# Stick-breaking scores of both heads from array rows 0 to 63 and 64 to 127, by chunks, with a changed start and mLSTM order

## The reference, cut to what matters

```
# mLSTM, 4 heads: keys and queries of 128, values of 256 (chunkwise in the reference)
s = einsum('bhts,...', qb, kb) * d
num = s @ v ;  den = sum(s) ;  h = num / max(abs(den), exp(-m)) ;  then rms_norm over the head, a gate, @ w_out

# stick-breaking, 16 heads of 64
z = einsum('bhtd,bhsd->bhts', qb, kb) * scale
log_1m = where(strict, log_sigmoid(-z), 0)
suffix = cumsum(log_1m, axis=3, reverse=True) - log_1m
a = where(strict, exp(log_sigmoid(z) + suffix), 0) ;  o = a @ v ;  o @ w_out
```

## Time and profile before

| what | us |
|---|---|
| median of 3 runs (2336.14 to 2337.36) | 2336.24 |
| the profiled execution's own time | 2334.94 |
| its span in the trace | 2333.6 |
| PE busy in the span | 2297.6 (98%) |
| DVE, ACT, POOL busy | 1042.0, 891.3, 1104.6 |

### The profile page before, as it was taken

The page is one execution under the profiler, slowest core; times in us unless marked ns, Lnnn a source line. Parts: engine busy times, 40 slices in busy tenths (PEclk is TensorE's granted clock), DMA queues, the critical chain, the costliest instruction groups (busy, mean ns, idle before and its releaser), DMA issues.

```text
span 2333.6 us, 31191 instructions
## 1 busy us (share of the span) xinstructions
PE 2297.6 (98%) x12833; PEld 1968.5 (84%) x12833; DVE 1042.0 (45%) x1521; ACT 891.3 (38%) x1322; POOL 1104.6 (47%) x833
## 2 busy tenths in 40 slices
PE   8999999999999999999999999999999999999998
PEld 6776888888888987778888888889999999999887
DVE  3138745622210614766564222018676446755402
ACT  4335643522222424746434222225345234322321
POOL 5335844444445352058335444555445444544453
PEclk9999999999999999999999999999999999999999
DMA  4222412222233242324123322323112222222232
GB/s 166 86 68 73 162 64 82 91 91 99 91 104 103 91 140 84 82 91 163 55 73 108 98 92 99 100 91 118 64 46 68 87 94 88 91 93 98 93 107 73
DMA packets 69054, 219.68 MB, mean 94 GB/s; under 512 B 9840, under 2 KB 14064, under 8 KB 68912
## 3 DMA queue, kind: packets, MB, share of 16 engines
q1 hardware_dynamic: 64160, 214.26, 28.2%
q10 hardware_dynamic: 4752, 3.42, 0.5%
HBM read 207.29 MB, written 2.10 MB: 90 GB/s over the span
## 4 chain that ended last, share of the span: by engine, by line
PE 92%; DVE 5%; ACT 2%; issue 1%; DMA 0%; SPq 0%; DVEq 0%; ACTq 0%
PE ps L443 76%; PE ps L572 6%; PE ps L958 2%; PE ps L996 1%; PE ps L737 1%; PE ps L761 1%; DVE x L1701 1%; DVE sp_lo L2139 1%; DVE ps L1699 1%; PE ps L467 1%; DVE u_lo L1680 1%; DMA w_land<-in_units 0%; DVE sp_hi L2137 0%; PE ps L658 0%; DVE arena L2135 0%
## 5 line engine op out<-in xcount | busy, mean ns | idle before, releaser
L2407 POOL TENSOR_TENSOR w_lo<-w_land,w_hi 128x512 fp32r<-128x512 f32 x768 | 1045.2, 1388 | 1106.3 <-ACT w_hi L1093 1105.5
L443 PE MATMUL ps<-u_hi,w_hi 128*128 128x512 f32 (+3 forms) x2360 | 755.0, 346 | 13.2 <-DVE u_lo L1680 12.8
L443 PE MATMUL ps<-u_lo,w_hi 128*128 128x512 f32 (+3 forms) x2360 | 750.9, 344 | 0.0
L443 PE MATMUL ps<-u_hi,w_lo 128*128 128x512 f32 (+3 forms) x2360 | 748.3, 343 | 0.0
L1093 ACT ACTIVATE w_hi<-w_land 128x1024 fp32r<-128x1024 f32 x384 | 401.1, 1051 | 249.6 <-DMA w_land<-in_units 247.0
L443 PEld LDWEIGHTS ps<-u_hi,w_hi 128*128 128x128 f32 x2360 | 420.2, 188 | 76.9 <-DVE u_lo L1680 15.3
L443 PEld LDWEIGHTS ps<-u_lo,w_hi 128*128 128x128 f32 x2360 | 417.8, 188 | 56.3 <-issue 1.4
L443 PEld LDWEIGHTS ps<-u_hi,w_lo 128*128 128x128 f32 x2360 | 418.5, 188 | 55.2
L443 PE MATMUL ps<-hid_hi,w_hi 128*128 128x512 f32 (+1 forms) x594 | 220.2, 371 | 0.0
L443 PE MATMUL ps<-hid_lo,w_hi 128*128 128x512 f32 (+1 forms) x594 | 219.7, 370 | 0.0
L443 PE MATMUL ps<-hid_hi,w_lo 128*128 128x512 f32 (+1 forms) x594 | 219.4, 369 | 0.0
(11 more groups left out here) (376 smaller groups left out, 3140.3 us busy)
## 6 DMA issues: line engine op xcount, KB each, us to landing
w_land<-in_units SPq DMA_DIRECT2D x384, 512.0 KB, 3.3
x<-in_xT SPq DMA_DIRECT2D x4, 528.0 KB, 7.1
arena<-in_memT ACTq DMA_DIRECT2D x2, 1024.0 KB, 5.3
outT<-x SPq DMA_DIRECT2D x16, 128.0 KB, 1.7
sb_split<-sb_split SPq DMA_DIRECT2D x14, 128.0 KB, 2.7
sb_q_lo<-sb_q_lo SPq DMA_DIRECT2D x13, 128.0 KB, 2.3
sb_split<-sb_q_lo SPq DMA_DIRECT2D x8, 128.0 KB, 2.4
sb_k_lo<-sb_split SPq DMA_DIRECT2D x6, 128.0 KB, 3.3
```

The costliest lines, as they stand in the source:

```text
L443: ins = pe.matmul(ps[:, bank, at:at + c1 - c0], w, rhs(k, c0, c1)[which], start=first and h == 0, stop=last and h == 2)
L2407: pool.tensor_tensor(w_lo[:, u % LAND, half], w_land[:, u % LAND, half], w_hi[:, u % RING, half].bitcast(F32), ALU.subtract).then_inc(*uni ...
```

## The change

**Start.** The first two units and x are loaded in smaller pieces, in the order in which they are needed: a half of unit 0, a tile of x, a half of unit 1, and so on; ACT's own queue loads the vectors. ACT rounds the halves between tiles of x, POOL subtracts them by halves, and PE's `first_head` takes unit 1 two tiles behind unit 0. Ahead of it PE multiplies zeros six times.

**mLSTM.** The three additions of `weights_sum` go from POOL to DVE; PE does the next head's scores and the sum of squares of the head before between the two halves of a numerator; the decays' arguments of heads 2 and 3 are made earlier, into a buffer of their own; DVE's and ACT's steps of the norm change places around this.

**Stick-breaking.** Nothing is stacked any more: the 63 copies by SP and their waits go, and `z` forms three products for every pair, of rows 0 to 63 for head 0 and 64 to 127 for head 1, alternating from one matmul to the next. For pairs 1 to 7 the work goes by chunks of both heads: PE does chunk 0 of both, then chunk 1 of both; ACT's exponentials go in that order; `z` waits for the exponentials of a chunk of both heads. POOL takes the two additions of head 1 and the rounding copies of chunk 1 of both heads.

```diff
+CHAIN = ((slice(SB_AT[2] + P, SB_AT[2] + 2 * P), slice(SB_AT[3], SB_AT[3] + P)),
+         (slice(SB_AT[1] + P, SB_AT[1] + 3 * P), slice(SB_AT[2], SB_AT[2] + 2 * P)))
...
+WARM = 6
+X_LOADS = ((0,), (1,), (2,), (3,), (4,), (5,), (6, 7))
+X_LOAD = (0, 1, 2, 3, 4, 5, 6, 6)
...
-        STACKED = {0: split_hi[0:4], 1: split_hi[4:8], 3: u_tiles(6) + u_tiles(7), 4: split_hi[0:4], 5: split_hi[4:8],
...
+        NATURAL = [split_hi[2 * i:2 * i + 2] for i in range(4)] + [u_tiles(i) for i in range(4, SB_H // 2)]
...
+            def first_head(name):
+                u0, u1 = UNIT[name], UNIT[name] + 1
+                begun[0] = 3
+                for k in range(UT):
+                    if k >= 2:
+                        if k == 2:
+                            pe.wait_ge(*unit_lo.at(2))
+                        if k == 6:
+                            pe.wait_ge(*unit_lo.at(4))
+                        tile(u1, k - 2, k - 2, u_rhs, ONE, four(1), k == 2, False)
+                    if k == 0:
+                        pe.wait_ge(*unit_lo.at(1))
+                    if k == 4:
+                        pe.wait_ge(*unit_lo.at(3))
+                    pe.wait_ge(*u_lo_at.at(step(0, k)))
+                    ins = tile(u0, k, k, u_rhs, ONE, four(0), k == 0, k == UT - 1)
+                ins.then_inc(*unit_done.up())
...
-                head(0, "ml_q", four, 2)
+                pe.wait_ge(*warm_set.at(1))
+                busy(7, sq[:, 0, 0:P], sq[:, 0, 0:2 * P], WARM)
+                first_head("ml_q")
...
+                        if n:
+                            if 1 <= h < ML_H - 1:
+                                scores(h + 1)
+                            if h:
+                                square_sum(h - 1)
...
-                    if 1 <= h < ML_H - 1:
-                        scores(h + 1)
...
+                def z(heads, i):
+                    q_hi, k_hi = NATURAL[i]
+                    products = ((k_hi, q_hi), (k_hi, q_tile(i)), (k_tile(i), q_hi))
+                    pe.wait_ge(*sb_split.at(SPLITS_BEFORE[i]))
...
-                            pe.wait_ge(*(sb_a0, sb_a)[n].at(2 * (i - 1) + h + 1))
+                            for h in heads:
+                                pe.wait_ge(*(sb_a0, sb_a)[n].at(2 * (i - 1) + h + 1))
                         for b in blocks:
                             for at, (k_, q_) in enumerate(products):
...
+                                for h in heads:
+                                    R = slice(64 * h, 64 * h + 64)
+                                    pe.matmul(block(h, b), k_[R, b * P:(b + 1) * P], q_[R, b * P:S],
+                                              start=b != 1 and at == 0, stop=False, skip_group_check=True)
+                        for h in heads:
...
-                    pe.wait_ge(*sb_lo_at.at(2 * at + 1))
+                    pe.wait_ge(*sb_lo_at.at(4 * i + (1 + h if i else 1 + 2 * h)))
...
+                def sums_first(h, i):
+                    at = 2 * i + h
                     pe.wait_ge(*sb_sp.at(2 * at + 2))
                     for part in (sp_hi, sp_lo):
                         pe.matmul(block(h, 0, P), neg_ones, part[:, h, SB_AT[1]:SB_AT[1] + S - P],
                                   start=False, stop=False, skip_group_check=True)
-                    pe.wait_ge(*sb_lo_at.at(2 * at + 2))
+                    pe.wait_ge(*sb_lo_at.at(4 * i + (3 + h if i else 2 + 2 * h)))
...
-                        sums(0, i)
-                    sums(1, i)
+                        sums_beside(0, i)
+                    sums_beside(1, i)
+                    if i:
+                        sums_first(0, i)
+                    sums_first(1, i)
                     if i + 1 < SB_H // 2:
-                        z(0, i + 1)
-                        z(1, i + 1)
+                        z((0, 1), i + 1)
...
+                act.dma_start(vecs[:, :], vecs_d).then_inc(*vecs_loaded.up(16))
                 table("natural_log_exp_and_others")
-                hi_to(EARLY)
+                def early_hi(n):
+                    u, c = n % 2, half_unit(n // 2)
+                    act.wait_ge(*early_landed[n].at(16))
+                    act.activation(w_hi[:, u, c], w_land[:, u, c], ACT.Copy).then_inc(*(early_hi_at if n < 2 else unit_hi).up())
+                early_hi(0)
                 act.wait_ge(*vecs_loaded.at(16))
                 act.wait_ge(*eps_set.at(1))
                 for k in range(DT):
+                    if 1 <= k < 4:
+                        early_hi(k)
                     upper_step(0, k)
                 hi_to(4)
...
+                    if h == ML_H - 1:
+                        rstd_head(h - 1)
...
-                    for h in range(2):
-                        for n in range(2):
-                            weights(h, i, n)
+                    for h, n in ((0, 0), (1, 0), (0, 1), (1, 1)):
...
+                def weights_sum(h):
+                    w, s_ = ml_w[:, h % 2, :], w_sum[:, h % 2, :]
+                    dve.wait_ge(*emptied_at["ml_s", h])
...
+                    if h == ML_H - 1:
+                        normed(h - 1)
...
+                    if h + 2 < ML_H:
+                        weights_sum(h + 2)
+                    if h < ML_H - 1:
+                        mean_square(h)
...
+                        if n == 0 and h and i:
+                            dve.wait_ge(*sb_chain.at(i))
+                        else:
+                            dve.wait_ge(*sb_sp.at(2 * (2 * i + h) + n + 1))
+                        if n == 0 and not (h and i):
+                            for to, from_ in CHAIN:
+                                dve.tensor_tensor(sp_[:, h, to], sp_[:, h, to], sp_[:, h, from_], ALU.add).then_inc(*dve_own.up())
                                 own()
...
-                        dve.tensor_copy(hi, v).then_inc(*dve_own.up())
-                        own()
+                        if n and i:
+                            dve.wait_ge(*sb_cast.at(2 * i + h - 1))
+                        else:
+                            dve.tensor_copy(hi, v).then_inc(*dve_own.up())
...
-                        halves_of(0, i + 1)
-                        halves_of(1, i + 1)
+                        for n in range(2):
+                            for h in range(2):
+                                halves_of(h, i + 1, (n,))
...
-            def weights_sum(h):
...
+            for n in range(4):
+                u, c = n % 2, half_unit(n // 2)
+                pool.wait_ge(*(early_hi_at if n < 2 else unit_hi).at(n % 2 + 1))
+                pool.tensor_tensor(w_lo[:, u, c], w_land[:, u, c], w_hi[:, u, c].bitcast(F32), ALU.subtract).then_inc(*unit_lo.up())
...
+            for i in range(1, SB_H // 2):
+                for h in range(2):
+                    if h:
+                        pool.wait_ge(*sb_sp.at(2 * (2 * i + h) + 1))
+                        pool.tensor_tensor(sp_[:, h, CHAIN[0][0]], sp_[:, h, CHAIN[0][0]], sp_[:, h, CHAIN[0][1]], ALU.add).then_inc(*pool_own.up())
+                        pool.wait_ge(*pool_own.now())
+                        pool.tensor_tensor(sp_[:, h, CHAIN[1][0]], sp_[:, h, CHAIN[1][0]], sp_[:, h, CHAIN[1][1]], ALU.add).then_inc(*sb_chain.up())
+                    pool.wait_ge(*sb_sp.at(2 * (2 * i + h) + 2))
+                    pool.tensor_copy(sp_hi[:, h, SB_PART[1][0]:SB_PART[1][1]], sp_[:, h, SB_PART[1][0]:SB_PART[1][1]]).then_inc(*sb_cast.up())
...
-            sp.dma_start(vecs[:, :], vecs_d).then_inc(*vecs_loaded.up(16))
-            for n in range(DT // 2):
-                if n < EARLY:
-                    unit_in(n)
-                sp.dma_start(x[:, 2 * n:2 * n + 2, :], xk[:, 2 * n:2 * n + 2, :]).then_inc(*x_loaded[n].up(16))
+            for n, ks in enumerate(X_LOADS):
+                if n < 4:
+                    u, c = n % 2, half_unit(n // 2)
+                    sp.dma_start(w_land[:, u, c], units[u, :, c]).then_inc(*early_landed[n].up(16))
+                sp.dma_start(x[:, ks[0]:ks[-1] + 1, :], xk[:, ks[0]:ks[-1] + 1, :]).then_inc(*x_loaded[n].up(16))
...
-                for to, from_ in moves[stage]:
-                    sp.dma_start(to.bitcast(F32), from_.bitcast(F32)).then_inc(*sb_stacked.up(16))
```

More of the change, by code:

```diff
@@ L350, in build @@
         unit_hi, unit_lo, unit_done = sem("unit_hi"), sem("unit_lo"), sem("unit_multiplied")
-        x_loaded = [sem(f"x_loaded{n}") for n in range(DT // 2)]
+        x_loaded = [sem(f"x_loaded{n}") for n in range(len(X_LOADS))]
         vecs_loaded, consts_loaded, gates_loaded, mem_loaded, mix_loaded, stored = (
@@ L356, in build @@
         act_own, dve_own, pool_own = sem("act_own"), sem("dve_own"), sem("pool_own")
-        eps_set = sem("eps_set")
+        eps_set, warm_set = sem("eps_set"), sem("warm_set")
+        early_landed, early_hi_at = [sem(f"early_landed{n}") for n in range(4)], sem("early_hi")
+        half_unit = lambda h: slice(h * UT * P // 2, (h + 1) * UT * P // 2)
```

(50 more changed lines are left out.)

126 lines of the change are left out of this document (39 added, 87 removed).

## The result

The changed kernel takes **2341.04 us** as a median of 19 runs (2338.75 to 2345.88), against 2336.24 before, also 19 runs (2334.7 to 2340.92): a ratio of 1.0015, 95% interval 1.0009 to 1.0021. That is slower beyond the noise, and the median is 0.4 us from the predicted 2341.4. But the two medians are 4.8 apart (0.21%), while the ratio amounts to 3.5, under the 0.2% that the prediction took as the least that can be told. Of 21 more runs of before, beside e1 to e4, the five above 2339 have a mean granted clock of 0.995 or 0.996 and the other 16 of 0.997 or 0.998, so the spread of these times goes with the clock. The profiled execution took 2342.84, 7.9 above the one of before (2334.94). It divides differently from the sum of the prediction, so the traces are read stage by stage first.

The account below looks back on a forecast made before the run. PE, busy 98%, was taken as the bound, except in the stick-breaking loop, where ACT, DVE and PE take turns. Terms -3.6 - 2.5 + 2.6 + 8.7 = +5.2 gave a median of 2341.4 us, range 2327 to near 2350 (forecast's own 2338 to 2346).

Parts of the forecast that it names:

- Start, -3.6: Start: `ml_k` was to begin at 32.0 instead of 35.7, about 3.6 us gained, bounds -2.0 and -5.0.
- mLSTM, -2.5: mLSTM: work between a numerator's halves was to cover waits of 0.95 and 1.75, about 2.5 us gained.
- First scores, +2.6: Pair 0's scores beside `sb_v`: unstacked, formed one head at a time without help from alternating, 2.6 us lost.
- The loop, +8.7: Stick-breaking, pairs 1 to 7: seven periods of 12.2 us against 76.7 before, 8.7 us lost; the deciding term.
- c: Loop: time of POOL's copy of 512 columns, taken as 0.85 us, between 0.42 and 1.27.
- 10.5 + 2c: Loop: period in us, adding up DVE's and POOL's work in order, then PE's tail; 12.2 was forecast.
- a short copy: Loop rival: c of 0.42 to 0.7, period 11.3 to 11.9, median 2335.4 to 2339.3 us; chance 0.25.
- a step costed at nothing: Loop: scores were taken as covered; chunk 0's 1.8 us were to end before the table load, costing nothing.
- E: Loop: the end of a pair's last exponential, from which the times within a period are counted.
- POOL and DVE don't hold each other up: Loop rival: no mutual slowing in these operations, period 10.1, the loop -6.0, median 2326.7 us; chance 0.20.
- Row halves don't run side by side: Loop rival: chunk 0's scores take 3.5 us, softplus 1.4 late, period 13.6, median 2351.2 us; chance 0.12.
- the estimate from that page: Loop: with the page's 769 ns for POOL's copy, a period of 12.0, a term of +7.6, 2340.3 us.

Follow-up runs that it names:

- e1: The changed start and mLSTM with the stick-breaking part as before: 2333.2 us, ratio 0.9981 to before.
- e4: The changed kernel plus eight matmuls of constants in PE's wait between head 0's and head 1's sums of chunk 0: 2337.86 us, ratio 1.0001 to before.
- e3: The changed kernel with POOL's two additions and its copies back on DVE: 2329.51 us, ratio 0.9965 to before.
- e7: The changed kernel with POOL doing only the copies of chunk 1, head 1's additions back on DVE: 2335.76 us, one execution.
- e10: As e3, with POOL doing the same kinds of operations on data that nobody uses: 2349.47 us, one execution.
- e9: The changed kernel with softplus for chunk 0 of both heads first and POOL's additions ahead of its two copies: 2333.94 us, ratio 0.9985 to before.
- e8: As e3, with softplus for chunk 0 of both heads, then chunk 1 of both: 2328.72 us, ratio 0.9958 to before.
- e2: Start and mLSTM as before, with the changed stick-breaking: 2345.3 us, ratio 1.0032 to before.
- e5: As e3, with a chunk's unstacked scores for head 0 first, then head 1, not alternating: 2335.22 us, ratio 0.9987 to before.
- e6: The changed kernel with POOL doing only head 1's two additions, the copies of chunk 1 back on DVE: 2333.44 us, one execution.
- e12: As e8, with two matmuls of head 0's chunk 1 sums moved into PE's wait: 2329.41 us, ratio 0.9959 to before.
- e11: As e3, without the six warm-up matmuls of zeros at the start: 2330.12 us, ratio 0.9971 to before.

## Why the prediction was right, and where only by a sum of errors

**Start, -3.6:** -3.4 measured, and by the mechanism named, `rstd` behind units 4 and 5. Both ends of the difference were too early by about the same: `ml_k` before began at 36.23 and not 35.7, after at 32.69 and not 32.0.

**mLSTM, -2.5:** -2.2. Both waits went; a wait of 0.68 that the prediction did not have came at the second head's scores.

**First scores, +2.6:** +2.7. The single halves of PE's rows get no cover, as argued.

**The loop, +8.7:** +10.6 in the profiled execution. From the first load to the end of the last exponential it was 76.7 (920.83 to 997.54) and is 87.3 (917.79 to 1005.13). But that has two parts. At the full clock it is 7 x 11.62 - 76.7 = +4.6, about half of the term. The mis-sized number is c, POOL's copy of 512 columns, taken as 0.85; it is 0.61 where DVE's copy gave way to it, and 0.75 where it met DVE's first copy. The formula 10.5 + 2c with 0.61 gives 11.7, near the 11.62. That is by its numbers the rival "a short copy", whose 2335.4 to 2339.3 hold the median of e4, 2337.86; its trace has no falls in the loop.

The mechanism behind the term, that POOL and DVE slow each other, is shown by e3, e7 and e10. Of the order in which I added things up, one piece was wrong: the first copy on POOL did not stand in DVE's way with its whole length (DVE's copy beside it took 0.56, and only the subtraction behind gave way, by 0.29), and in its place came the wait of head 1's softplus behind head 0's chunk 1 (e9: 0.5 a period). Part of that wait is a step costed at nothing: chunk 1's scores, for which ACT waits 0.44. So it is partly luck that the formula comes near 11.62. As measured, POOL's additions begin at E + 3.93 and take 1.14 and 0.74, then DVE's copy takes 0.93 and its subtraction 0.96, to E + 7.85. Without the 0.69 and the 0.37 by which the first addition and the copy are longer, this would be E + 6.79, an estimate from these rows, about e3's 6.73. So POOL's share saves nothing even undisturbed, and the lengthening is its cost.

The other part, some 6 in the profiled execution, is the clock. The prediction counted PE's longer wait for halves as time that costs nothing beyond itself, and named no fall of the clock at all. e4 shows that filling that wait removes it; between the medians it is 3.2. This missed term and the too large c (8.7 - 4.6 = 4.1) nearly cancel, so that 2341.4 came so near is luck.

**The rivals.** "POOL and DVE don't hold each other up" is refuted by e10; its price was too good besides, since it had POOL's additions done at E + 4.6, and they begin only at E + 3.93. "Row halves don't run side by side" is refuted by the trace; the Trainium skill's page "TensorEngine Tiling (Array Packing)", section "Theoretical Speedup", with up to twice for 64 rows, is agreed with here by 18 matmuls in 1.42 us, where the 9 of one head alone took about as long in `sb_v` (883.09 to 884.48, 1.39). The page "GPSIMD Engine Reference" of the Trainium skill, section 3.1, gives 769 ns for 512 elements of a tight loop; the copy of 512 columns took 0.61 here where nothing held it up, so the estimate from that page was too high as well.

## What to carry to other kernels

Work that is moved to an idle engine isn't free when both engines work on SBUF at the same moment: here 2.4 us of POOL's work (by its undisturbed lengths) made a chain 1.1 longer, though DVE had less to do. Price a wait of the matmul engine not only by its length: the clock may fall behind it, as e4 showed by filling it, and then it costs as much again. And look at the sum of a right forecast by its terms before believing its reasons; a version without POOL's share (e3, e8) is about 0.4% faster than before.

## What the runs showed of the hardware that was not expected

- The clock fell after PE's waits of 1.6 to 1.7 us in some periods and not in others, with the same program and the same wait (963.62 and 952.00 above). It then ran at half speed for 3.6 us or more. The wait of 1.73 for the exponentials of pair 0 was followed by a fall in e2, e5, e6, e10 and e12, and by none in the changed kernel, e3, e4, e7, e8, e9 and e11. Behind the waits of 1.2 in e7 none of the seven periods has one. In e1 the clock fell with PE busy throughout, near 928.7, some 6 us after a wait of 1.08 that ended at 922.62 (two windows of e1, ahead of the fall and in it). Why one wait has it and its twin has not is left open.

```profile
922.62:925.52 2.90, 2.90 (x17) 2.45 (x18) 2.83 (x6) 1.36 (x2) 0.00 (x0) 1.00 0.58 136
929.00:933.00 4.00, 4.00 (x13) 2.17 (x14) 3.83 (x8) 1.62 (x3) 0.00 (x0) 0.50 0.52 121
```

- Behind a fall a period is 1.4 to 1.5 longer in the changed kernel, 2.4 in the first of e5, and 3.1 in pair 2 of e1, where PE has no slack.
- At the very start matmuls lie 0.43 apart while the granted clock's column reads 1.00, and so in e11. That column doesn't show the slow beginning.
- POOL's copy of 512 columns takes 0.61, half of its subtraction with two inputs (1.27), and POOL's addition of 128 columns can take 1.14 instead of 0.45 beside DVE's subtraction. In the rows of the changed kernel, the one that begins second is longer by what is left of the first, less about 0.15: DVE's subtraction at 947.62 by 0.29, with 0.44 of POOL's copy left; POOL's addition at 948.03 by 0.69, with 0.84 of that subtraction left; DVE's copy at 950.02 by 0.37, with 0.52 of POOL's second copy left. The one that began first keeps its length. e6 agrees: 0.41, with 0.55 left. The page "SBUF — State Buffer" of the Trainium skill, section "Who interferes with whom", speaks of an exclusive lock on a pair of ports that the two engines share; these rows agree, but for the 0.15.
